# Other orders of the first projection and of the sparse attention, and products of the identity at the waits of four norms, two softmaxes and the router

## The reference, cut to what matters

```python
# first block, each layer
hx = norm_modulate(x, norm1_g[i], sh1, sc1)      # rms_norm(x, g) * (1 + scale) + shift
q, k, v = jnp.split(hx @ w_in, splits, axis=-1)
p = softmax_f32(jnp.einsum('bqhgd,bkhd->bhgqk', q, k) * scale)
x = x + g1 * ox
x = x + g2 * conv_ffn(norm_modulate(x, norm2_g[i], sh2, sc2), ...)
# second block, second layer
yc = _nsa(q, kc, vc, ks, vs, kw, vw, gl, ...)    # compressed, selected and window branch
h = h + jnp.concatenate([yc, yd], axis=-1) @ o_w_out[i]
hn = _rms_norm(h, o_norm_ffn[i])
logits = xf @ w_router + b_router                # top 2 of 8 experts, softmax of the two
h = h + _moe_swiglu(hn, ...)
```

## Time and profile before

| | us |
|---|---|
| median of 3 runs | 2070.64 |
| lowest, highest | 2067.16, 2074.06 |
| the profiled execution | 2077.58 |
| its span, first to last instruction | 2075.7 |

### The profile page before, as it was taken

How to read it: one execution, slowest core, us unless ns; L and a number is a source line. 1 busy time by engine, 2 the same in 40 slices (tenths; PEclk the granted TensorE clock), 3 DMA queues, 4 the chain that set the end, 5 groups by cost and what they waited for, 6 DMA issues and landing times.

```text
span 2075.7 us, 32710 instructions
## 1 busy us (share of the span) xinstructions
PE 1947.7 (94%) x13400; PEld 1659.5 (80%) x13400; DVE 1334.4 (64%) x2036; ACT 1073.5 (52%) x1744; POOL 280.0 (13%) x291
## 2 busy tenths in 40 slices
PE   6999889999999899899999889999988899999998
PEld 3675568888787785899998888999877688888886
DVE  2338545676545558677667556545666688888886
ACT  2346533333334466466555425444445577676774
POOL 1201123010100300332111412111101000000000
PEclk9999999999999899999999999999998999999998
DMA  8332443554222220245553113555542489889794
GB/s 320 127 137 103 163 175 109 183 183 183 110 85 90 88 102 21 89 177 183 203 184 141 43 38 121 200 183 203 202 165 72 177 326 341 324 319 349 303 346 164
DMA packets 52812, 364.81 MB, mean 176 GB/s; under 512 B 5936, under 2 KB 8240, under 8 KB 8880
## 3 DMA queue, kind: packets, MB, share of 16 engines
q1 hardware_dynamic: 50304, 359.68, 46.9%
q10 hardware_dynamic: 2352, 2.96, 0.5%
HBM read 361.57 MB, written 1.05 MB: 175 GB/s over the span
## 4 chain that ended last, share of the span: by engine, by line
PE 82%; DVE 8%; ACT 4%; issue 3%; POOL 2%; DMA 1%; SPq 0%; DVEq 0%; POOLq 0%; ACTq 0%
PE ps L77 22%; PE ps L78 21%; PE ps L79 21%; PE ps L74 15%; DVE WLO L91 3%; PE ps L82 2%; ACT R L85 2%; ACT WHI L85 1%; DVE SM L105 1%; POOL R L91 1%; DMA ring<-W 1%; DVE R L91 1%; POOL h L95 0%; DVE h L88 0%; DVE x L88 0%
## 5 line engine op out<-in xcount | busy, mean ns | idle before, releaser
L91 DVE TENSOR_TENSOR WLO<-ring,WHI 128x1024 fp32r<-128x1024 f32 x566 | 682.2, 1240 | 194.5 <-ACT WHI L85 193.9
L85 ACT ACTIVATE WHI<-ring 128x1024 fp32r<-128x1024 f32 x566 | 577.8, 1052 | 101.7 <-PE ps L79 98.0
L77 PE MATMUL ps<-HHI,WHI 128*128 128x256 f32 (+1 forms) x1584 | 514.4, 325 | 32.2 <-DVE HLO L88 18.0
L78 PE MATMUL ps<-HLO,WHI 128*128 128x256 f32 (+1 forms) x1648 | 526.1, 319 | 0.0
L79 PE MATMUL ps<-HHI,WLO 128*128 128x256 f32 (+1 forms) x1584 | 507.9, 321 | 0.0
L77 PEld LDWEIGHTS ps<-HHI,WHI 128*128 128x128 f32 x1584 | 305.1, 193 | 75.2 <-issue 29.0
L78 PEld LDWEIGHTS ps<-HLO,WHI 128*128 128x128 f32 x1648 | 316.1, 192 | 23.0
L79 PEld LDWEIGHTS ps<-HHI,WLO 128*128 128x128 f32 x1584 | 303.8, 192 | 24.3
L74 PE MATMUL ps<-R 64*64 64x64 f32 (+10 forms) x2448 | 192.7, 291 | 4.5 <-ACT R L85 2.5
L85 ACT ACTIVATE R<-ps,VEC 128x512 f32<-128x512 f32 (+1 forms) x106 | 69.3, 658 | 244.1 <-PE ps L79 242.0
L91 POOL TENSOR_TENSOR R<-R 128x256 f32<-128x256 f32 (+1 forms) x99 | 108.4, 1098 | 544.8 <-ACT R L85 543.6
(11 more groups left out here) (220 smaller groups left out, 2994.6 us busy)
## 6 DMA issues: line engine op xcount, KB each, us to landing
ring<-W SPq DMA_DIRECT2D x340, 1024.0 KB, 4.9
x<-xt SPq DMA_DIRECT2D x2, 1024.0 KB, 6.7
out<-x SPq DMA_DIRECT2D x2, 512.0 KB, 3.9
CR<-const_nsa ACTq DMA_DIRECT2D x1, 560.0 KB, 3.7
CR<-const_rw ACTq DMA_DIRECT2D x1, 448.0 KB, 3.4
CR<-const_gqa ACTq DMA_DIRECT2D x1, 320.0 KB, 10.3
CR<-const_mla ACTq DMA_DIRECT2D x1, 320.0 KB, 2.9
VEC<-vec ACTq DMA_DIRECT2D x1, 314.0 KB, 10.1
```

What stands on the lines that cost most here:

```text
L77: self.e.matmul(out, l[0], r[0], start=start, stop=False)
L78: self.e.matmul(out, l[0], r[1], start=False, stop=False)
L85: return self.e.activation(out, in_, func, **kw)
L91: return self.e.tensor_tensor(out, in0, in1, op)
```

## The change

1. `warm(pe, n)`: n products of the identity with itself, 128 columns each, into the bank that is next in turn, which nobody reads. They stand in `tail_pe` ahead of the last sum, behind it, and behind the spread, in numbers given for each norm by `WARM`; in both softmaxes ahead of the first turn (12 and 8); in the router ahead of the places (5) and ahead of the first gather (5). `tail_pe` of norm 2 has 0 ahead of its last sum, which leaves the wait for the bank.
2. First projection: the parts of job 1 ahead of the slices 1 (three) and 2, the turn ahead of slice 3. DVE makes the first slice's low part before it scales the second. High and low parts of the weight units are spread over the walk one by one.
3. Sparse attention: ACT's four high units go one to each of the steps 2 to 5, behind the exponential. The four low units go from DVE to POOL, ahead of its other work there, under a semaphore of their own.

```diff
--- before.py
+++ after.py
@@ -639,6 +639,17 @@
         S.events["bank", label] = i
         return ps[i]
 
+    def warm(pe, n):
+
+        i = turn_of[0]
+        if i in freed_by:
+            pe.wait_ge(*at(*freed_by[i]))
+        pe.wait_ge(*at("d_c0"))
+        for _ in range(n):
+            pe.mm(ps[i][:, 0:128], ident, ident, True, True)
+
+    WARM = {1: (4, 3, 12), 2: (0, 4, 12), 5: (8, 3, 8), 10: (8, 3, 3)}
+
     def keep(i):
 
         turn_of.remove(i)
@@ -669,6 +680,14 @@
             src = ring[:, (c % RING) * SLOT + col:(c % RING) * SLOT + col + UNIT]
             e.tt(WLO[:, o:o + UNIT], src, WHI[:, o:o + UNIT], ALU.subtract).then_inc(
                 *did("w_lo", ("lo", u)))
+
+    def lo_units_pool(g, units):
+        for u in units:
+            c, col, _, _ = F.units[u]
+            o = (u % UNITS) * UNIT
+            g.wait_ge(*at("hi", u))
+            src = ring[:, (c % RING) * SLOT + col:(c % RING) * SLOT + col + UNIT]
+            g.tt(WLO[:, o:o + UNIT], src, WHI[:, o:o + UNIT], ALU.subtract).then_inc(*did("w_lo_pool", ("lo", u)))
 
     def split_of(p, o=0):
         return WHI[:, p.at:p.at + p.cn], WLO[:, p.at:p.at + p.cn]
@@ -901,11 +920,14 @@
             if k < n["tiles"]:
                 for s in segs:
                     scale_dve(v, c, k, s)
-            if n["split"] and k >= 1 and by_dve(c, k - 1):
+            if n["split"] and k >= 1 and by_dve(c, k - 1) and (c or k > 1):
                 for s in segs:
                     low_dve(v, c, k - 1, s)
             if between:
                 between(k)
+            if (c, k) == (0, 0):
+                for s in segs:
+                    low_dve(v, c, 0, s)
 
     def apply_act(a, c, between=None):
         n = NORM[c]
@@ -988,11 +1010,14 @@
 
 
     def tail_pe(pe, c):
+        warm(pe, WARM[c][0])
         sum_pe(pe, c, NORM[c]["tiles"] - 1)
+        warm(pe, WARM[c][1])
         if c == 7:
             double_pe(pe)
         else:
             spread_pe(pe, c)
+        warm(pe, WARM[c][2])
 
     def tail_act(a, c, nxt, made=0):
         hi_units(a, nxt.first[made:2])
@@ -1635,9 +1660,9 @@
     def gqa_pe(pe):
         st, steps = L["gqa_in"], L["ada0"]
         def second_job(k):
-            for s in {1: (0, 1), 2: (2,), 3: (3,)}.get(k, ()):
+            for s in {1: (0, 1, 2), 2: (3,)}.get(k, ()):
                 ada_part_pe(pe, L["ada_pe"][4 + s], 1, s)
-            if k == 4:
+            if k == 3:
                 ada_turn_pe(pe, 1)
                 give(bank_of["rs", 0])
 
@@ -1775,6 +1800,8 @@
         for i in range(A.n + 2):
             if i + 1 < A.n:
                 A.scores_pe(pe, i + 1)
+            if i == 1:
+                warm(pe, 12 if A is gqa else 8)
             if 1 <= i <= A.n:
                 A.turn_pe(pe, i - 1)
             if i >= 2:
@@ -3223,10 +3250,10 @@
 
     def nsa_act(a):
         for i in range(11):
-            if i == 6:
-                hi_units(a, L["o_out"].first)
             if 1 <= i < 8:
                 nsa_exp_act(a, i)
+            if 2 <= i < 6:
+                hi_units(a, L["o_out"].first[i - 2:i - 1])
             if 2 <= i < 10:
                 nsa_copy(a, i - 2, 1)
             if i >= 4 and i % 2 == 0:
@@ -3234,8 +3261,6 @@
 
     def nsa_dve(v):
         for i in range(1, 10):
-            if i == 7:
-                lo_units(v, L["o_out"].first)
             if i < 8:
                 nsa_max_dve(v, i)
             if 2 <= i <= 8:
@@ -3244,6 +3269,7 @@
                 nsa_copy(v, i - 2, 0)
 
     def nsa_pool(g):
+        lo_units_pool(g, L["o_out"].first)
         for f in range(4):
             g.wait_ge(*at("oh", f))
             g.tt(HLO[:, f, 0:256], h[:, f, 0:256], HHI[:, f, 0:256], ALU.subtract).then_inc(
@@ -3287,6 +3313,7 @@
                     for i in range(2):
                         t = pe.mm(b[:, 8 * i:8 * i + 8], LR[:, 128 * i:128 * i + 128], SEL8, True, True)
                     t.then_inc(*did("group", ("router",)))
+        warm(pe, 5)
         b = take(pe, ("place",), ("flag0",))
         pe.wait_ge(*at("two"))
         pe.wait_ge(*at("d_cr", "moe"))
@@ -3416,6 +3443,8 @@
         st = L["moe", r]
 
         def gather(p):
+            if p == 0:
+                warm(pe, 5)
             for e in (2 * p, 2 * p + 1):
                 pe.wait_ge(*at("places", r, e))
             for i, name in enumerate(("hi", "lo")):
@@ -3770,9 +3799,11 @@
         first_squares_act(a)
         root_act(a, 0)
         ada_row_act(a, 0, None)
-        hi_units(a, L["gqa_in"].first[0:2])
+        hi_units(a, L["gqa_in"].first[0:1])
 
         def second_job(k):
+            if k == 1:
+                hi_units(a, L["gqa_in"].first[1:2])
             if k == 3:
                 ada_row_act(a, 1, 0)
                 hi_units(a, L["gqa_in"].first[2:4])
@@ -3832,12 +3863,14 @@
         ada_job_dve(v, 0)
 
         def second_job(k):
+            if k in (0, 2):
+                lo_units(v, L["gqa_in"].first[k // 2:k // 2 + 1])
             if k == 3:
-                v.wait_ge(*at("mod0", 0, 0))
                 ada_job_dve(v, 1)
-                lo_units(v, L["gqa_in"].first[2:4])
+                lo_units(v, L["gqa_in"].first[2:3])
                 v.wait_ge(*at("mod", 0, 1))
-        lo_units(v, L["gqa_in"].first[0:2])
+            if k == 5:
+                lo_units(v, L["gqa_in"].first[3:4])
         apply_dve(v, 0, [("mod", 0, 0)], second_job)
         gqa_dve(v)
```

## The result

The changed kernel takes 2064.27 us (median of 16 runs, 2060.86 to 2071.73), the kernel before, timed on the same chip, 2072.73 us (16 runs, 2065.68 to 2081.55). The ratio is 0.9961, 95% interval 0.9949 to 0.9973: 8.1 us faster, between 5.6 and 10.6. The forecast was 19.1 us, and its range ended at 2061. The sign was right and the size more than twice too large. So the size of the gain is known to within several us only.

The account below looks back on a forecast made before the run. It took TensorE (82% of the last chain), its waits and half-clock stretches to bound the kernel; its terms summed to -19.1 us, 2077.6 to 2058.5 profiled, 2051.5 for the timed median, range 2043 to 2061.

Parts of the forecast that it names:

- First projection: Reorder of the first projection: fifth slice begins 6.4 us earlier, at full clock; sum -7.3, between -5 and -8.5.
- of the 2.3 gained some 0.9 stay: First projection: fifth slice's products gain 2.3 us at full clock; the sixth waits for POOL (about 5.4), so 0.9 stay.
- gain taken back: Rival in the first projection: late chunks take back 5 of the 7.3 us, giving 2056.5; 6%.
- Sparse attention: Low units leave DVE for POOL, ACT's high units dealt one to a step: -6.4 us, between -4 and -7.
- The maximum comes 5.0 earlier: Sparse attention: without DVE's low-unit block the seventh step's maximum comes 5.0 us earlier; TensorE's wait shrinks to 1.3.
- POOL and DVE hindering each other: Rival in the sparse attention: POOL's low units take 5.8 us each, DVE's ops lengthen; -16 in all, 2054.5; 10%.
- Norm 1: Norm after the gqa output: products win 1.7 us, a grown wait for POOL costs 1.1; -0.6, between -1.9 and +1.
- mla: Softmax of mla: eight products exceed the 0.94 us wait and push dense work; +0.7, up to +3 at half clock.
- norm 2: Norm after the first down projection: products cost +1.0, POOL's pace decides later slices; sum 0, between -1.9 and +1.3.
- norm 5: Norm after the mla output: products fill the waits, sum, spread and first slices gain clock; -2.2, between -2.5 and +0.5.
- router and gather: Router and gather at full clock, first expert product 1.5 us earlier; -2.4 in all, between -3.2 and +1.
- the products buy no clock: Rival: clock falls anyway or the identity does not count, only the reorders act; -11, 2059.5; 15%.

Follow-up runs that it names:

- e5: Changed kernel with the low halves of the first projection's sixth slice on DVE instead of POOL; 0.9943 of the kernel before, 11.8 us faster.
- e4: Changed kernel without the products of the identity, so both reorders alone; 0.9971 of the kernel before, 6.0 us faster.
- e7: Changed kernel with ACT's high units behind the sparse attention's copies and eight identity products ahead of the turn of step 7; 0.9981 of the kernel before.
- e12: Changed kernel without the identity products in norm 1, norm 2 and the mla softmax; 0.9942 of the kernel before, 12.0 us faster.
- e1: Kernel before with the reorder of the first projection alone; 0.9986 (0.9968 to 1.0003), 2.9 us faster.
- e2: Kernel before with the moves of the sparse attention alone; 0.9990 (0.9973 to 1.0007), 2.1 us faster.
- e10: Changed kernel once more, unchanged; 2062.27 us, 0.9932 (0.9912 to 0.9952) of the kernel before.
- e3: Kernel before with the identity products alone, at all their places, no reorder; 0.9980 (0.9967 to 0.9993), 4.1 us faster.
- e6: Changed kernel with the second slice's low halves of norms 1, 2 and 5 on DVE instead of POOL; 0.9950 of the kernel before, 10.4 us.
- e8: Changed kernel with twelve identity products ahead of the first slice of the first projection; 0.9948 of the kernel before, 10.8 us faster.
- e9: Changed kernel with the edits of e5, e6 and e8 and no products in the mla softmax; 2049.72 us, 0.9881 of the kernel before.

## Why the prediction was right or wrong

**First projection (-7.3, measured -2.0).** The first half of the step was right: the fifth slice 6.2 earlier in the profiled pair (forecast 6.4), its wait 1.17 (1.3), at full clock. The step that failed is "of the 2.3 gained some 0.9 stay". From the fifth slice to the group behind the sums it is 29.8 us instead of 26.0 before: 3.8 lost instead of 0.9 gained. Before, the fifth slice ran at half clock, and that hid POOL's steps for the sixth. I took them at 5.4, as before; now they take 6.6, the first of them 2.37 instead of 1.24, with a low unit of DVE beside it. So the sixth slice begins 6.1 behind the fifth instead of 5.3, and the wait of 3.07 drops the clock: 1.3 more are lost in the slices six to eight, and 1.6 where the clock falls once more, over the sums at 76.0. e5 took POOL out of this place and won 3.4 in the four slices. That the second fall lies over the sums is a matter of the single execution, and costs hardly anything of itself: in e4, e7 and e12 the sums run at full clock, but the first slow stretch is 6.8 us long and the slices six to eight take 11.2 to 11.4 instead of 9.9. Where the slow time falls hardly matters: from the fifth slice on it is 29.5 to 30.0 in all seven profiles of the table with this reorder, and 25.8 to 26.0 in all four without. The rival "gain taken back" had the size nearly right (5 of 7.3) and the cause wrong: no chunk is waited for.

**Sparse attention (-6.4, measured -2.9; -3.7 in the profiled pair).** "The maximum comes 5.0 earlier" failed. The block of the earlier trace rows lasts 5.14 from 1575.49, but the maximum behind it waits for the turn of two steps back as well, and in the kernel before those transposes ended at 1576.59. The maximum could not have begun before 1576.7; it began at 1580.56. So 1.2 of the block cost nothing, the maximum comes 3.9 earlier, and the wait shrinks by 3.8. The rest: the copies behind the high units cost 0.5 and 0.2 (forecast up to 0.3), and of the clock either 1.2 are lost ahead of the last wait and 1.4 won behind it (two profiles of nine, the profiled pair's among them) or neither (seven). POOL was right: 2.35 a low unit (2.5), each done long before it is wanted. The rival of POOL and DVE hindering each other was wrong for POOL's own time here. DVE did pay once: a step of 128x4 took 0.88 beside a low unit of POOL, and 0.17 else.

**Norm 1 (-0.6, measured +0.8).** I foresaw the wait for POOL (3.3; it is 3.09) and the fall of the clock in it (+1.1; it is 1.5). What failed is the -1.7 on the other side: that last sum and spread run at half clock before. That was so in the profile I had, but not in e1, e2 and e4, and even in the first, where the second slice came 1.5 earlier, the fall took these 1.5 back: 34.87 before, 34.86 after. One profile was not enough to call this a property of the kernel.

**The others held within 0.3:** gqa -1.05 (-0.9), mla +0.6 (+0.7), norm 2 +0.3 (0), norm 5 -2.0 (-2.2), router and gather -2.3 (-2.4). The price of a product was 0.24 (0.22). The rival that the products buy no clock is right in norms 1 and 2, where a wait for POOL comes behind, and wrong elsewhere.

**The range.** The bounds of the terms were taken from each place alone. The first projection's lower bound, -5, left no room for the case that the sixth slice's wait eats all that the fifth gains, though the earlier trace rows had POOL's 1.69 beside 0.73. The Trainium skill (GPSIMD Engine Reference, Key points) says that GpSimd shares its SBUF interfaces with VectorE and contends with those of its instructions that have two SBUF inputs (or run in a 2-port mode); by that rule the forecast's own rival belonged here, in the first projection. The rows agree on that: 2.37 against 0.93 for the same step beside DVE's low halves and low unit, which read two tensors of SBUF, and 0.74, as alone, beside its scalings, which read one and PSUM. No run varied DVE's work alone.

**What is not in any term.** The profiled pair differs by 14.0, the table's terms by 11.0 for that pair. Some 3.9 of the rest is the second up projection at the faster of the two paces; two stretches at half clock behind it (1293.8 and 1495.2 before, 3.4 us each) are missing, though e10 has them again. Against that stands a cost. From norm 1's eighth slice to norm 2 it is 362.7 in both profiles of the kernel before and 366.0 in both of the changed kernel, with no line changed there. The first down projection has the same waits of 3.31 and 2.01 in both kernels; before, the clock did not fall at either, after it falls in the one and right behind the other, for 6.8 and 3.4 us. e3, e6 and e7 have 366.0 too and e5 364.8, the other six 363.0 to 363.3. So some 3 us of what the change wins in its own places is lost there in most kernels with the products in norm 1; what decides it is open, since e8 and e9, which have them too, take 363.1 and 363.3. The forecast has no term for it, and took it that time won at a place reaches the end.

## What to carry to other kernels

A gain on the way to one slice is worth only as much as the next slice's producer lets through: before counting it, lay the slowest helper engine's steps for the following slice beside the new, earlier start, at the durations that they have next to a busy neighbour. Filling a wait to keep the clock paid where all waits behind it were filled or hidden too (norm 5, the gather, e8); where one of 3 us follows, the slow stretch only moved out of waiting and into work (norm 1), and the helper's steps are to be moved first (e6, e9). When a block of work leaves an engine, what is won is the time to the next input's arrival, not the block's length; look at all events that the next instruction waits for, also those that only free a buffer.

A sum of local terms misses what the change does to the clock elsewhere: compare the sections between the edits too, in two profiles of each kernel at least.

## What the runs showed of the hardware

The same dense products of 256 columns run at one of two paces while the granted clock is 1.00: 80 us of the second up projection held 709 in the changed kernel and 682 in e5, whose code is the same there.

```profile
903.00:983.00 80.00, 80.00 (x709) 80.00 (x708) 64.49 (x89) 53.85 (x89) 22.33 (x30) 1.00 0.55 191
```

```profile
900.00:980.00 80.00, 80.00 (x682) 80.00 (x681) 62.06 (x86) 51.80 (x86) 21.54 (x29) 1.00 0.53 189
```

That is 113 or 117 ns each. The pace holds for tens of microseconds at a time, and the pattern differs between executions of one kernel (427 against 444 products in 50 us, at e10). It is worth 3.9 us in the second up projection, and accounts for part of the spread of the times. What chooses the pace stays open; no run here was made for it.

A wait of one length drops the clock in some executions and not in others: the waits of 3.31 and 2.01 in the first down projection left it at full in both profiles of the kernel before; in both of the changed kernel it fell in the first and right behind the second.
